# A hybrid encoder step: first maxima and last query plane sooner, a gate product ahead of the last outputs, down weights over the prompt rows

## The reference

```python
qa, ka, va, qb, kb, vb, iq, ik, iw, ga, gb = split_projection(rmsnorm(xp, g_attn), w_in)
oa = window_attn_prompt(qa, ka, va, attn_sink, bias_a)
ob = dsa_prompt(qb, iq, iw, kb, vb, ik, bias_b)      # top-k keys of relu(iq ik) * iw

merged = sigmoid(ga) * dot(oa, w_branch_a) + sigmoid(gb) * dot(ob, w_branch_b)
x = x + dot(merged, w_out)
# moe: best of 4 groups, best 2 of its 8 experts, weights wts
#   out = dot(silu(dot(h, w_gate[e])) * dot(h, w_up[e]), w_down[e])
x = x + moe_ffn(rmsnorm(x, g_ffn), ...)
x = x + sigmoid(dot(rmsnorm(x, g_ple), w_ple_gate)) * dot(p, w_ple)
y = rmsnorm(x, g_final)
```

## Time and profile before

| | us |
|---|---|
| median of 3 runs | 1027.2 |
| lowest and highest run | 1026.95, 1031.04 |
| the profiled execution | 1030.55 |
| its span, first to last instruction | 1028.5 |
| PE busy | 920.1 |
| DVE busy | 377.5 |
| ACT busy | 259.0 |
| POOL busy | 141.4 |
| bytes moved by DMA | 263.72 MB |

### The profile page before, as it was taken

The page is one execution under the profiler, slowest core; times in us unless marked ns, Lnnn a source line. Parts: engine busy times, 40 slices in busy tenths (PEclk is TensorE's granted clock), DMA queues, the critical chain, the costliest instruction groups (busy, mean ns, idle before and its releaser), DMA issues.

```text
span 1028.5 us, 14275 instructions
## 1 busy us (share of the span) xinstructions
PE 920.1 (89%) x5750; PEld 588.0 (57%) x5750; DVE 377.5 (37%) x967; ACT 259.0 (25%) x526; POOL 141.4 (14%) x146
## 2 busy tenths in 40 slices
PE   7999999999999999998999887887887887888996
PEld 6969994457999998983333322222222222334775
DVE  4279997854233354352111110101101001103796
ACT  6354318664231242231000000000000000001542
POOL 2705432122110000001111111011010011000000
PEclk9999998999999999998999999999999999999998
DMA  9860602005633406377999999999999999995601
GB/s 266 114 159 1 206 1 62 1 2 150 202 105 103 124 1 267 109 284 265 426 427 427 425 428 428 423 427 425 429 427 427 426 427 426 427 426 243 256 22 66
DMA packets 60132, 263.72 MB, mean 256 GB/s; under 512 B 11054, under 2 KB 36030, under 8 KB 46224
## 3 DMA queue, kind: packets, MB, share of 16 engines
q1 hardware_dynamic: 54160, 250.99, 63.6%
q0 software_dynamic: 5296, 9.79, 2.6%
q10 hardware_dynamic: 624, 2.23, 0.6%
HBM read 253.99 MB, written 16.85 MB: 263 GB/s over the span
## 4 chain that ended last, share of the span: by engine, by line
PE 54%; DMA 30%; DVE 12%; ACT 2%; issue 2%; SPq 1%; DVEq 0%; ACTq 0%
DMA arena<-in_w_up 26%; PE ps L1163 13%; PE ps L1330 12%; PE ps L1195 4%; PE ps L1478 4%; DVE nrm L2013 3%; PE ps L1355 3%; DVE hT L2017 3%; DMA arena<-in_w_ple 2%; PE ps L941 2%; PE ps L1089 2%; PE ps L1110 2%; PE ps L1059 2%; PE ps L1451 1%; PE ps L1224 1%
## 5 line engine op out<-in xcount | busy, mean ns | idle before, releaser
L1330 PE MATMUL ps<-arena,hT 128*64 128x512 f32 x960 | 234.4, 641 | 39.6 <-DMA arena<-in_w_up 39.4
L1330 PEld LDWEIGHTS ps<-arena,hT 128*64 128x64 f32 x960 | 71.0, 141 | 200.1 <-issue 148.4
L2284 DVE TENSOR_TENSOR xf<-xf,ps 128x256 f32<-128x256 f32 x32 | 13.5, 421 | 401.9 <-ACT xf L1771 379.3
L1163 PE MATMUL ps<-arena_merge,arena_merge 128*128 128x256 f32 x624 | 99.7, 287 | 0.0
L851 POOL DMA_INDIRECT expert_rows<-xf,arena x32 | 32.1, 1002 | 426.2 <-ACT xf L1775 400.4
L1355 PE MATMUL ps<-arena,xf 128*64 128x512 f32 x336 | 76.7, 598 | 12.8 <-DVE xf L2287 12.8
L1163 PEld LDWEIGHTS ps<-arena_merge,arena_merge 128*128 128x128 f32 x624 | 87.5, 188 | 0.0
L1163 PE MATMUL ps<-xf_merge,arena_merge 128*128 128x256 f32 x480 | 82.0, 288 | 0.0
L1771 ACT ACTIVATE xf<-ps 128x256 f32<-128x256 f32 x30 | 11.5, 384 | 259.5 <-PE ps L1330 259.5
L1163 PEld LDWEIGHTS ps<-xf_merge,arena_merge 128*128 128x128 f32 x480 | 69.3, 188 | 0.0
L1775 ACT ACTIVATE xf<-ps 128x512 f32<-128x512 f32 x30 | 17.9, 597 | 159.8 <-PE ps L1355 159.8
(11 more groups left out here) (313 smaller groups left out, 1309.0 us busy)
## 6 DMA issues: line engine op xcount, KB each, us to landing
arena<-in_w_gate SPq DMA_DIRECT2D x30, 2048.0 KB, 29.6
arena<-in_w_up SPq DMA_DIRECT2D x30, 2048.0 KB, 36.9
arena<-in_w_down SPq DMA_DIRECT2D x11, 2048.0 KB, 36.1
hT<-in_w_down SPq DMA_DIRECT2D x11, 2048.0 KB, 36.8
arena<-in_w_down SPq DMA_DIRECT2D x20, 1024.0 KB, 31.2
arena<-in_w_in SPq DMA_DIRECT2D x10, 1024.0 KB, 6.2
arena<-in_w_in SPq DMA_DIRECT2D x3, 2048.0 KB, 10.6
arena<-in_w_gate SPq DMA_DIRECT2D x8, 512.0 KB, 9.0
```

Source lines behind the costliest of these rows:

```text
L1163: mm = pe.matmul(w[:, 2 * lo_t:lo_t + hi_t], rounded(st[:, c, cols]), rounded(mv[:, c, lo_t:hi_t]), start=c == 0 and k == 0, stop=c == pla ...
L1330: mm = pe.matmul(ps[g * BLK:(g + 1) * BLK, 2 + s, :], xsT[:, c, col:col + BLK], expert_columns(k, slice(0, 2), c, g), start=c == 0, stop=c ...
```

## The change

Four parts.

1. *Attention's start.* `row_max` of units 0 to 3 comes ahead of DVE's last two rounds of selection before attention (`MAXIMA_LATER`). Of the last query plane ACT copies only the first half, now behind the exponential of unit 3; DVE copies the other at the start of its part of attention. PE waits for DVE's half before the scores of units 6 and 7.
2. *The first gate product.* PE's wait for `ot_out` stands behind it.
3. *Down weights over the prompt rows.* `x_nat`, tiles 0 to 3, becomes a fourth place for down weights, used once, for expert 3. SP loads it by quarters, each when its tile has been turned and scaled. From expert 4 on the place is (e - 1) % 3. SP's, and PE's, first pass of the loop is written out. Behind the loop, SP loads the rows back from `normed_rows`. These are scaled by the norm's factor r, so the experts' weights `wts` are multiplied by r, 1/r is kept in `nrm` (`UNIT`), and the later squares, norms and the last addition of the rows carry 1/r. p and w_ple move to another tile, the turned rows to the places of p and w_ple.
4. *Gains.* g_attn's load counts on the sample rows' semaphore; the two other gains are loaded behind the constants.

```diff
@@ DVE, selection and attention
+        for b in BLOCKS:
+            for k in range(SELECT_FIRST if b == 's' else TOPK_P // 8):
+                if b == 's' and k == SELECT_FIRST - MAXIMA_LATER:
+                    dve.wait_ge(toep_ready, 2)
+                    for u in range(4):
+                        row_max(u)
...
-        dve.wait_ge(toep_ready, 2)
-        row_max(0)
+        dve.wait_ge(wide_full, WIDE[('qa', QA_ORDER[-1])].fill)
+        h = 2 * QA_ORDER[-1] + 1
+        dve.tensor_scalar(by_half(qx[h // HG * HD:(h // HG + 1) * HD, h % HG, :]), banks(wide(3), HD, P), -HD ** -0.5, None,
+                          ALU.mult).then_inc(wide_out['dve'], 1)
         for u in range(len(UNITS) + WEIGH + 1):
-            if u + 1 < len(UNITS):
+            if 4 <= u + 1 < len(UNITS):
                 row_max(u + 1)
@@ ACT, attention
-            if u == 2:
-                queries_out('qa', QA_ORDER[-1])
             act.wait_ge(max_ready, u + 1)
             v = pr[u % len(pr)][:, 0:keys + (br == 'a')]
             act.activation(v, v, ACT.Exp, bias=stat[:, 0, g, j:j + 1], scale=-1.0,
                            accum_out=stat[:, 1, g, j:j + 1]).then_inc(exp_done, 1)
+            if u == 3:
+                queries_out('qa', QA_ORDER[-1])
@@ PE
+            if u == 4:
+                pe.wait_ge(wide_out['dve'], WIDE_DONE['dve'] + 1)
...
-        pe.wait_ge(ot_out, len(GROUP_UNITS))
         for q in range(CHUNKS):
...
                 w = wide(open_slot(LATE, ('b' + br, m), late_out))
+                if q == 0 and j == 0:
+                    pe.wait_ge(ot_out, len(GROUP_UNITS))
@@ places
+    w_dn.append([x_nat[:, c:c + 1, :] for c in range(4)])
+    def dn_place(e):
+        return e if e < PLACES + 1 else (e - 1) % PLACES
@@ SP
+        def load_dn_over_rows(t):
+            i = ROUTE.index(t)
+            sp.wait_ge(xf_ready, i + 1)
+            sp.wait_ge(turn_full, i + 1)
+            load(x_nat[:, t, :], A['w_down'][0, PLACES].rearrange("(p h) n -> h p n", h=4)[t], dn_in[PLACES])
+        load_dn_over_rows(0)
+        load_dn_over_rows(1)
         sp.wait_ge(rows_full, 4)
...
+        load_dn_over_rows(2)
         sp.wait_ge(part_used, 1)
...
         load_planes(2, 1, 3, 5)
+        load_dn_over_rows(3)
...
+        def next_down(k, e):
             sp.wait_ge(dn_done, e - (PLACES - 1))
             load_dn(k, e)
+        for e in range(PLACES, PLACES + LOOP):
+            next_gate_up(e % PLACES, e)
+            if e > PLACES:
+                next_down(dn_place(e), e)
...
         load(w_pg[:, 0:KD // 2], w_pg_d[:, 0:KD // 2], w_pg_in[0])
+        sp.wait_ge(xn_stored, 16 * 4)
+        load(x_nat[:, 0:4, :], xn_d[0:NP].rearrange("(t p) n -> p t n", p=P), x_in[0])
@@ DVE, weights of the experts and behind the loop
+        link(dve.tensor_tensor(wts[:, :, 1:2], wts[:, :, 0:1], rt_e21, ALU.mult))
+        link(dve.tensor_tensor(wts[:, 0:4, :], wts[:, 0:4, :], nrm[:, 5:9].unsqueeze(2).to_broadcast([P, 4, 2]), ALU.mult))
+        dve.reciprocal(nrm[:, UNIT:UNIT + 4], nrm[:, 5:9])
...
+            link(dve.tensor_tensor(v[:, 0:hi - lo], v[:, 0:hi - lo], nrm[:, UNIT + lo:UNIT + hi], ALU.mult))
...
-                dve.tensor_tensor(x_nat[:, t, :], x_nat[:, t, :], sgl[t], ALU.add).then_inc(x4_ready, 1)
+                dve.scalar_tensor_tensor(x_nat[:, t, :], x_nat[:, t, :], nrm[:, UNIT + t:UNIT + t + 1], sgl[t], ALU.mult, ALU.add)\
+                    .then_inc(x4_ready, 1)
```

More of the change, by code:

```diff
@@ L282, in _program @@
         twin(arena, "front", int(lo * 256), int(hi * 256))
[L283 removed]
+    for lo, hi in ((0, 32.5), (70.5, 78.5), (80, 112), (131.25, 139.25)):
         twin(arena, "gate", int(lo * 256), int(hi * 256))
@@ L1367, in pair @@
                 gate_up(s, k, s * BLK).then_inc(gu_done, 1)
-                if s == 0 and more:
-                    pe.wait_ge(xs_in[(j + 1) % 3], i * 16 + (16 + (j + 1) // 3 * 16))
+                if s == 0:
+                    pe.wait_ge(xs_in[(j + 1) % 3], i * 16 + 16 * ((body * BODY + j + 1) // 3 + 1))
                     rows_turned((j + 1) % 3).then_inc(xsT_full, 1)
@@ L1381, in _ @@
         keep_busy(1)
-        with pe.Fori(0, BODIES) as i:
+        for j in range(BODY):
+            pair(0, 0, j)
+        with pe.Fori(0, BODIES - 1) as i:
             for j in range(BODY):
-                pair(i, j, True)
+                pair(i, 1, j)
         p, k, use = PAIRS - 1, (EXPERTS - 2) % PLACES, (EXPERTS - 2) // PLACES + 1
@@ L1533, in _ @@
         for t in range(TILES):
-            act.wait_ge(x_in[t], 16)
+            act.wait_ge(x_in[t], 16 if t < 4 else 32)
             r = ROWS[t]
@@ L1610, in queries_out @@
             act.wait_ge(wide_full, WIDE[(q, m)].fill)
-            for s in range(2):
+            for s in range(2 if (q, m) != ('qa', QA_ORDER[-1]) else 1):
                 h = 2 * m + s
@@ L1819, in gate_weights_high, with unit @@
                 .then_inc(w_pg_high, 1)
+        def unit(t):
+            return nrm[:, UNIT + t:UNIT + t + 1] if t < TILES - 1 else 1.0
         def third_squares(i):
@@ L1824, in third_squares @@
             act.wait_ge(x3_ready, i + 1)
-            act.activation(yo[t][0:n, :], x_nat[0:n, t, :], ACT.Square, accum_out=nrm[0:n, 10 + i:11 + i])\
+            act.activation(yo[t][0:n, :], x_nat[0:n, t, :], ACT.Square, scale=unit(t), accum_out=nrm[0:n, 10 + i:11 + i])\
                 .then_inc(x3_squares, 1)
```

101 lines of the change are left out of this document (57 added, 44 removed).

## The result

The changed kernel takes 1021.33 us (median of 9 runs, 1019.61 to 1022.66), the kernel before 1027.73 beside it (9 runs, 1025.29 to 1031.13). The ratio is 0.9933 with a 95% interval of 0.9916 to 0.9950: 6.9 us gained, 5.1 to 8.6. Forecast were 5.2 us and 1022.0. The two profiled executions lie further apart than that: spans of 1028.5 and 1017.9, so 10.6 us. Most of this document is on where these 10.6 us are, and which of them belong to the change.

The account below looks back on a forecast made before the run. DMA bounds the expert loop and PE's products nearly everything else. Gains of 0.9, 0.86 and 3.7 less 0.25 us of cost make 5.2, taken from a median of 1027.2: 1022.0 us, range 1019.0 to 1025.5.

Parts of the forecast that it names:

- Maxima and query plane: Start of attention: earlier maxima and a plane copy shared by ACT and DVE gain 0.9 us, bounds 0.3 to 1.8.
- rival 1: Start of attention: PE's clock does not fall there, another 2 us gained, time 1020.0; chance 0.27.
- Gate product: End of attention: the first gate product starts ahead of the wait for the last outputs; gain 0.86 us.
- Quarters: Ahead of the expert loop: three of four quarter loads of expert 3's down weights cost nothing; gain 3.7 us.
- The stock: Expert loop, load issued at 494.90: 5 to 6 us stood ahead of it, 2 left after the change.
- The return of the rows: Behind the loop: loading the prompt rows back ahead of the gathers costs 0, upper bound 1.7 us.
- the cover of 1.3 us: Behind the loop: two additions end at 958.5 and PE turns these rows at 959.76, 1.3 us to spare.
- Rival 2: Behind the loop: gathers queue behind the rows on slow DMA engines, PE's turn 1.7 us late, 1023.7; chance 0.13.
- The last weights: End of the loop: the last weights land some 5.4 us sooner in the new profile.
- Small costs: Behind the loop: tiny DVE products cost 0.2 us and three-operand last additions 0.05, together 0.25 us.
- Rival 3: Expert loop: quarters fill no idle time or stock runs dry near 495; half of 3.7 lost, 1023.9; chance 0.13.
- rival 4: Behind the loop: rows land late, PE stands still, its clock falls; costs 10.6 us, time 1032.6; chance 0.03.

Follow-up runs that it names:

- the changed kernel again: The changed kernel with no line changed, timed in another group: 1021.49 us, ratio 0.9943.
- gains alone: The kernel before with only the fourth part, two of the three gain loads behind the constants: 1029.23 us, ratio 1.0013.
- split return: The changed kernel with the rows' return cut in four, tile 0 ahead of the gathers, tiles 1 to 3 each before its own: 1020.49 us, ratio 0.9922.
- the two fillers: Two identity products put into PE's gap behind the last down product, on top of the split return: 1019.99 us, ratio 0.9923.

## Why the prediction was right, point by point

**Maxima and query plane: right.** 0.9 us forecast, 0.87 measured, the scores 7.64 us behind the first ones in ten profiles. The maxima come 3.1 us sooner behind the first scores in nine of them and 4.3 in the tenth (the changed kernel again), which makes no difference to the scores. The bounds of 0.3 to 1.8 were not needed.

**The clock fall where attention begins: rival 1, and it came in a form that I had not thought of.** I took the fall as a fixed thing that the change may or may not remove. It is one that strikes in some executions. The new start was free of it in ten profiles of ten, the old one in two of four, and the times leave 1.9 us (with 1.9 either way) for it.

**Gate product: right.** 0.86 forecast, 0.93 measured, and no later stage loses it.

**Quarters: right in the mechanism, 0.5 too much in size.** The loop is 439.1 to 440.3 us with them in idle time (eight profiles with three quarters, mean 439.65) and 442.6 to 443.1 without (four, mean 442.8): 3.2 us against 3.7. The stock is the term that was mis-sized: I had 2 us left behind the three quarters, and the next quarter of 1.2 us found next to nothing. Whether the missing 0.5 is the stock's is not shown: in windows of 3 us at that place the changed kernel moves 406 to 422 GB/s, but such windows of the saturated stretch go from 391 to 448 in the kernel before. Against the same loads issued late (443.10) the idle time is worth 3.45 us.

**The return of the rows: this step failed.** The prediction's own sign for it came, the turn of the first rows waits (1.51 us). I took 0 with an upper bound of 1.7, and looked at the gathers, which would queue behind the rows. They do not. What the rows hold up is the last scatter, 4.7 to 6.0 us, and SP waits for it before it issues a gather. The Trainium skill, DMA: Bandwidth & Descriptors, section "Queues, rings and completion order", says that a transfer's signal of completion on a DMA engine lands only after every earlier write of that engine, across its queues; the runs agree so far, for the scatter is POOL's, the rows are SP's, and between 938 and 941 the engines' mean share is 0.21 while the scatter is still out. They do not show the rule itself: the scatter landed at 941.23, 2 us before the last of the rows at 943.25, so it did not wait for the whole load. The price is 18.62 - 17.60 = 1.0 us against the kernel with the old order and a clean clock (gains alone), 1.5 against the kernels without or with a split return. And the cover of 1.3 us, on which the 0 stood, was not there: in the earlier trace rows the turn comes late because PE's clock had fallen at 948 and the products of p took 12.93 us instead of 11.29. With a clean clock the turn comes 17.60 us behind the last down product, not 18.58. So the price hangs on the clock. Where it holds, the turn comes after 18.62 to 19.18 us with the rows in one piece (four profiles) and after 17.00 to 17.60 without or split (four), 1.6 less on the average. Where it falls behind the last down product, as in six of the fourteen, it comes after 18.58 and 19.13 with the rows in one piece and after 18.54 to 19.26 without or split (four), and the return costs nothing clear. Rival 2 had the right place and, at 1.7, nearly the right price, by the wrong transfer.

**The last weights** come 10.5 us sooner in the profiles (last down product at 930.72 instead of 941.18), where 5.4 were said: the 5.1 of the three steps, and the falls and the start.

**Small costs: right.** The stretch from the turn to PE's end is 59.48 against 59.31 and 59.28: 0.2 us for 0.25. The last stretch is 0.3 shorter in every kernel with the third part; I have no reason for it.

**Gains' loads: right,** 0.

**The sum.** Put together as measured: 0.87 + 0.93 + 3.2 - 1.0 - 0.2 + 0.3 = 4.1 us. The times gave 6.9 and 5.9. The forecast of 5.2 came out close by luck, since errors met: the return cost 1.0 and the loop gave 0.5 less, and on the other side stand about 2 us that the sum had left out. The clock at 159 is the likely source of most of them, and up to 0.9 may be the way to the first expert; the times can't part the two. The 1022.0 is nearer to the measured 1021.33 than the gain is to its own, for the kernel before took 1027.73 beside it and not the 1027.2 that I started from. Rival 3 did not happen (the loop lost 0.5, not 1.85), nor rival 4.

## What to carry to other kernels

Bytes that are moved out of a saturated stretch into idle DMA time shorten the program by nearly their own time (3.2 of 3.7 us here), but only as far as the stock of loaded work reaches; a window table of GB/s behind the start of the stretch shows at once when it is used up. A load that is put ahead of a last small transfer can delay that transfer's completion, even from another queue (here from 4.4 to 5.1 us to 6.0 to 6.2), so cut it and put ahead only the piece that is needed first. Before a wait or a cover is priced from one profile, look whether PE's clock was down in it: both the cover behind the experts and 3.8 us of the difference between the two profiles were made of such falls.

## What the runs showed of the hardware

The granted clock falls in different places in executions of the same code. The wait in the changed kernel:
```profile
384.68 0.39 PE L1238 MATMUL ps<-arena_merge,arena_merge 128*128 128x256 f32 x1 [1.02 <-DVE arena_merge L2176]
```
After this same wait at the start of the products with w_out, eleven of fourteen profiles stay at 1.00 and three fall, at 384 to 396; each of the three takes 68.34 us for these products and the others 66.84. Behind the last down product six of fourteen fall, at the start of the program eleven of fourteen. PE is not idle for more than 2.2 us ahead of any of these but the last. Thus the kernel before, whose runs in one group reach from 1024.8 to 1032.9, is hard to compare by its total with anything closer than 0.2%, about what the intervals above reach to either side; the distances between marks in the timeline tell 0.1 to 0.2 us where the clock holds.

The best of the kernels here are the changed one with its return split (1020.49, ratio 0.9922) and the same with the two fillers (1019.99, 0.9923). Between them the times decide nothing, and against the changed kernel (0.9933 and 0.9943) the intervals overlap as well; for the split speak the stages, 17.00 us to the turn instead of 18.62, in executions whose clock holds there.
